# The last stage of a one-core encoder layer: the two expert rows of each token are added to x by accumulating transfers instead of by VectorE and GpSimd

## The reference, cut to what matters

```
    x = x + jnp.concatenate([dsa_out, ml_out], axis=-1) @ w_out[layer]
    x = x + memory_cross_attn(rmsnorm(x, norm_x_g[layer]), mem_n, ...)
    x = x + hier_moe(rmsnorm(x, norm_ffn_g[layer]), ...)
return rmsnorm(x, final_norm_g)
```

## Time and profile before

| | us |
|---|---|
| median of 3 runs | 2610.08 |
| the profiled execution | 2609.71 |
| its span, first to last instruction | 2607.9 |
| last expert store landed | 2554.86 |
| first `fin_o` tile finished | 2588.22 |
| last `fin_o` tile finished | 2603.58 |

### The profile page before, as it was taken

The page is one execution under the profiler, slowest core; times in us unless marked ns, Lnnn a source line. Parts: engine busy times, 40 slices in busy tenths (PEclk is TensorE's granted clock), DMA queues, the critical chain, the costliest instruction groups (busy, mean ns, idle before and its releaser), DMA issues.

```text
span 2607.9 us, 31347 instructions
## 1 busy us (share of the span) xinstructions
PE 2373.8 (91%) x11141; PEld 1866.7 (72%) x11141; DVE 1530.6 (59%) x1704; ACT 1214.9 (47%) x1376; POOL 305.7 (12%) x182
## 2 busy tenths in 40 slices
PE   6999999989999999999998299999999999999990
PEld 6888588667889998885887276666666666666660
DVE  4322376564335543223223488888888888888875
ACT  4222333354323442223222266776776777776751
POOL 0000000000000000000000112222222222222222
PEclk9999999999999999999999699999999999999995
DMA  4333133202424653320433489999999999999985
GB/s 174 97 96 97 48 92 95 71 25 91 147 93 147 177 181 126 97 89 1 120 96 118 144 309 400 410 402 394 410 395 394 413 404 395 407 398 400 402 331 215
DMA packets 141965, 580.45 MB, mean 223 GB/s; under 512 B 24395, under 2 KB 26705, under 8 KB 86737
## 3 DMA queue, kind: packets, MB, share of 16 engines
q1 hardware_dynamic: 136528, 562.85, 57.9%
q0 software_dynamic: 5376, 16.81, 2.0%
HBM read 571.15 MB, written 25.23 MB: 229 GB/s over the span
## 4 chain that ended last, share of the span: by engine, by line
PE 61%; DMA 17%; DVE 12%; issue 5%; ACT 4%; POOL 0%; DVEq 0%; SPq 0%; ACTq 0%; POOLq 0%
PE psd L726 42%; DMA e_raw<-in_w_gate_dram 8%; DMA e_raw<-in_w_down_dram 7%; DVE e_lo L1916 5%; PE psx L1052 3%; PE psx L1053 3%; PE psd L1080 2%; ACT e_hi L1430 2%; DVE y_sb L2025 1%; PE psd L987 1%; PE psx L1037 1%; PE psx L968 1%; PE psx L762 1%; PE psx L1060 1%; ACT y_sb L1474 1%
## 5 line engine op out<-in xcount | busy, mean ns | idle before, releaser
L1916 DVE TENSOR_TENSOR e_lo<-e_raw,e_hi 128x2048 fp32r<-128x2048 f32 x320 | 721.2, 2286 | 138.3 <-ACT e_hi L1430 136.0
L1535 DVE TENSOR_TENSOR w_lo<-w_raw,w_hi 128x1024 fp32r<-128x1024 f32 (+1 forms) x240 | 291.0, 1213 | 642.4 <-ACT w_hi L1130 642.3
L1430 ACT ACTIVATE e_hi<-e_raw 128x2048 fp32r<-128x2048 f32 x320 | 602.1, 1912 | 88.3 <-DMA e_raw<-in_w_gate_dram 65.3
L1130 ACT ACTIVATE w_hi<-w_raw 128x1024 fp32r<-128x1024 f32 (+1 forms) x240 | 252.0, 1050 | 763.9 <-PE psd L726 763.9
L1052 PE MATMUL psx<-e_hi,xt_pair 128*128 128x512 f32 x1024 | 430.1, 420 | 67.1 <-DVE e_lo L1916 61.5
L1053 PE MATMUL psx<-e_lo,xt_pair 128*128 128x512 f32 x1024 | 418.2, 408 | 0.0
L726 PE MATMUL psd<-w_hi,act_hi 128*128 128x512 f32 (+1 forms) x832 | 320.7, 385 | 6.1 <-DVE act_lo L1591 2.0
L726 PE MATMUL psd<-w_hi,act_lo 128*128 128x512 f32 (+1 forms) x832 | 319.7, 384 | 0.0
L726 PE MATMUL psd<-w_lo,act_hi 128*128 128x512 f32 (+1 forms) x832 | 319.6, 384 | 0.0
L1052 PEld LDWEIGHTS psx<-e_hi,xt_pair 128*128 128x128 f32 x1024 | 204.1, 199 | 138.9 <-DVE e_lo L1916 90.8
L661 POOL DMA_INDIRECT y_rows<-y_sb,put_idx x32 | 208.6, 6517 | 588.8 <-DVE y_sb L2025 588.8
(11 more groups left out here) (305 smaller groups left out, 2932.5 us busy)
## 6 DMA issues: line engine op xcount, KB each, us to landing
e_raw<-in_w_gate_dram SPq DMA_DIRECT2D x128, 1024.0 KB, 11.3
e_raw<-in_w_up_dram SPq DMA_DIRECT2D x128, 1024.0 KB, 7.9
e_raw<-in_w_down_dram SPq DMA_DIRECT2D x128, 1024.0 KB, 10.0
w_raw<-in_w_in_dram SPq DMA_DIRECT2D x72, 512.0 KB, 3.6
w_raw<-in_w_ckv_dram SPq DMA_DIRECT2D x64, 512.0 KB, 3.7
w_raw<-in_w_out_dram SPq DMA_DIRECT2D x32, 512.0 KB, 3.6
w_raw<-in_w_cq_dram SPq DMA_DIRECT2D x32, 512.0 KB, 3.6
w_raw<-in_w_co_dram SPq DMA_DIRECT2D x32, 512.0 KB, 3.6
```

The lines of the kernel that those rows point to most:

```text
L1130: act.activation(w_hi[j % 2][:, :, 0:w], w_raw[j % 4][:, :, 0:w], ACT.Copy).then_inc(hi_done, 1)
L1430: act.activation(e_hi[n][:, :], raw_at(b, r)[:, :], ACT.Copy).then_inc(e_hi_done, 1)
L1535: dve.tensor_tensor(w_lo[j % 2][:, :, 0:w], w_raw[j % 4][:, :, 0:w], w_hi[j % 2][:, :, 0:w].bitcast(F32), ALU.subtract).then_inc(lo_done, 1)
L1916: dve.tensor_tensor(e_lo[n][:, :], raw_at(b, r)[:, :], e_hi[n][:, :].bitcast(F32), ALU.subtract).then_inc(e_lo_done, 1)
```

## The change

The tiles `y_back` and the two engines' additions go. GpSimd itself begins eight transfers of 1 MB with `accum_op=ALU.add`: each reads 128 rows of `y_rows` and adds them to a tile of `x_res` in place. The first four bring the first experts' rows (k = 0), one for each tile; the second four bring the second experts' rows (k = 1), and each waits until the first transfer into its tile has landed, since both add to the same bytes. ACT's square of tile t waits for `back_land[t]` at 32, that is for both. DVE only norms. GpSimd needs no word from SP to begin; SP's only load is `fin_gain`.

```
-        y_back = [at(f"y_back{t}", [P, 2, D], 16 * t) for t in range(TT)]
...
-        f_pair, f_add, f_sq, f_out = (sem(s) for s in ("f_pair", "f_add", "f_sq", "f_out"))
+        f_sq, f_out = (sem(s) for s in ("f_sq", "f_out"))
...
             sp.dma_start(fin_gain[:, :], final_norm_g.rearrange("(a d) -> a d", a=1).to_broadcast([P, D])).then_inc(fg_land, 16)
             for t in range(TT):
-                sp.dma_start(y_back[t][:, :, :],
-                             y_rows.rearrange("(k t p) d -> t p k d", k=2, p=P)[t]).then_inc(back_land[t], 16)
-            for t in range(TT):
                 sp.wait_ge(f_out, t + 1)
...
             pool.sem_inc(experts_done, 1)
 
-            for t in range(1, TT):
-                pool.wait_ge(back_land[t], 16)
-                pool.tensor_tensor(y_back[t][:, 0, :], y_back[t][:, 0, :], y_back[t][:, 1, :], ALU.add).then_inc(f_pair, 1)
+            for k in range(2):
+                for t in range(TT):
+                    if k:
+                        pool.wait_ge(back_land[t], 16)
+                    pool.dma_start(x_res[:, t, :], y_rows[T * k + P * t:T * k + P * t + P, :],
+                                   accum_op=ALU.add).then_inc(back_land[t], 16)
...
             for t in range(TT):
-                act.wait_ge(f_add, t + 1)
+                act.wait_ge(back_land[t], 32)
                 if t:
                     act.wait_ge(f_sq, t)
...
-            for t in range(TT):
-                if t == 0:
-                    dve.wait_ge(back_land[t], 16)
-                    link(dve.tensor_tensor(y_back[t][:, 0, :], y_back[t][:, 0, :], y_back[t][:, 1, :], ALU.add))
-                else:
-                    dve.wait_ge(f_pair, t)
-                dve.tensor_tensor(x_res[:, t, :], x_res[:, t, :], y_back[t][:, 0, :], ALU.add).then_inc(f_add, 1)
-                if t:
-                    finish(t - 1)
+            for t in range(TT - 1):
+                finish(t)
             finish(TT - 1)
```

## The result

The changed kernel takes 2618.02 us, the median of 19 runs; the kernel before, run beside it 19 times, 2611.53. The ratio is 1.0025, with a 95% interval of 1.0018 to 1.0033: 6.5 us slower, 4.7 to 8.6 by the interval. The forecast was 2618.

A forecast was written before the change was run, and what follows sets the result against it. The last stage was taken as bound by loads for 20 us, then by DVE and GpSimd. From 2554.9, adding 3.1, 2.5, 39.7, 5.0, 0.5 and 10.3 gave a 2616.0 us span, a time of 2618, range 2602 to 2639.

The forecast's parts named there:

- terms 1, 2: Start of the last stage: 3.1 us for start and landing of a GpSimd transfer, 2.5 us for loading `fin_gain`.
- term 3: Eight 1 MB accumulates in the last stage, each 4.96 us, twice a plain copy's time: 39.7 us.
- term 4: Output stores ahead of the last accumulate put off its landing: 5.0 us for tiles 0 and 1, 0.5 for the third.
- term 5: From the last landing to the end: ACT's square, DVE's norm of one tile, the store and program end, 10.3 us.
- two units: Each 1 MB accumulate takes twice a copy's 2.48 us, 4.96 us, giving a time of 2618; chance 45%.
- The prediction's other estimate: Sixteen engines at about 16.2 GB/s each accumulate at 259 GB/s: 4.05 us an accumulate, a time of 2611.
- The hidden waits: Second transfers' waits for the first into their tile, and GpSimd's issues of about 1 us, hide behind 15 us of queued work.
- The rival that feared 6.9 us: GpSimd's instruction bounds the eight accumulates at 6.9 us each, 55.2 us in all, a time of 2630; chance 5%.
- The faster side: Each of the eight accumulates costs only a copy's 2.48 us, DVE bounds the rest, a time of 2598; chance 13%.
- The point where its sign turns: The change neither gains nor loses when the eight accumulates take 32.1 us, 4.0 us each.

The follow-up runs named there:

- e1: The changed kernel with the addition left out of its eight transfers, so they only copy: ratio 0.9948 to the kernel before, stage 39.5 us.
- e3: The kernel before, but GpSimd first adds the second experts' rows to the first's in HBM, SP loads the sums, DVE adds them to x: ratio 1.0010.
- e9: e1 with each copy writing its destination as the rounded float32 type, so each element is converted: transfers 2.49 us apart, stage 40.2 us.
- e11: The changed kernel, unchanged, profiled a second time: span 2614.7 us, stage 58.4 us.
- e5: e4 with no output store begun before tile 3 has its last accumulate: ratio 1.0007 to the kernel before, stage 57.6 us.
- e4: The changed kernel with four buffers for the normed tiles in place of two: ratio 1.0023 to the kernel before, stage 57.7 us.
- e2: The kernel before with all additions on DVE and none on GpSimd: ratio 0.9977 to the kernel before, stage 47.5 us.
- e6: e2 with `fin_gain` loaded behind the second pair of rows: 2605.2 us, ratio 0.9973 to the kernel before, stage 45.0 us.

## Why the prediction was right, term by term

| term | forecast | measured |
|---|---|---|
| last expert store | 2554.9 | 2558.9 |
| start, fixed time and `fin_gain` (terms 1, 2) | 5.6 | 6.1 |
| eight accumulates (term 3) | 39.7 | 39.2 |
| output stores among them (term 4) | 5.5 | 2.3 |
| last landing to the end (term 5) | 10.3 | 10.8 |
| the stage | 61.1 | 58.4 |
| span | 2616.0 | 2617.3 |

The measured second row is the first landing, 11.0 us after the expert stores (2570.18 less 0.28 of issue, less 2558.86), less one accumulate of 4.9.

**Term 3 decided it, and held.** I took two units between the bounds of one and three, from full occupancy in the earlier trace rows; it is 4.90 against 2.48, a ratio of 1.98. The rule of the Trainium skill, "Collectives: The Full Stack", section "The bandwidth ceiling: the fold count and why AG ≠ RS ≠ AR", a ratio of 1.93 for its collectives, agrees with the trace. The prediction's other estimate from that section of the Trainium skill, 32.35 GB/s over the two engines that it counts, so 16.2 each and 259 for sixteen, does not: the stretches show 213 to 223. e1 and e3 take away the queue, the number of packets and the destination as causes; e9 takes away the elements' handling at least where they are converted.

**The hidden waits were hidden.** GpSimd's first four accumulates took 3.69 us of its own time together and the others 0.86 each, about L649's 0.97 in the earlier trace rows, and 4.9 us lie between landings across the step from the first four to the second. The rival that feared 6.9 us is gone.

**The faster side was priced rightly.** It said 2595.7 for copies that add, 40.8 us behind the expert stores; e1, with copies that don't, has 39.5. The point where its sign turns, 32.1 us for eight, leaves out the 0.5 of term 4; with it it is 31.6, still 4.0 each.

**Term 4 was mis-sized.** I gave each store a unit ahead of the last landing. Only one fell there: the intervals are 4.9, 4.9 and 7.2. The first store was issued at 2596.39, took 10.4 us to land beside the accumulates and came in at 2606.8, just behind the last of them; the second landed later still. The changed kernel's two queues (GpSimd's q0, SP's q1: packets, MB, share) from 2597 to 2600 and from 2600 to 2606:

```profile
q0 software_dynamic: 88, 0.59, 95.1%
q1 hardware_dynamic: 7, 0.06, 4.7%
```

```profile
q0 software_dynamic: 104, 0.75, 59.7%
q1 hardware_dynamic: 120, 0.97, 39.9%
```

For 3.6 us after its issue the store hardly moved, and then the stores moved more bytes than the accumulates. I had let it begin at once. What holds it back at first stays open; e11 has the same (0.02 MB in the first 3.6 us). The prediction also has the first store begin 6.3 us after its tile's landing, where the parts of term 5 give 5.9; it began 6.9 after it (2596.39 - 2589.48), since about 1 us of tile 0's table load showed. e5 shows the size in another way: without any store the last landing is 1.9 us earlier.

**What I had not named:** the wait for a store before tile 2 may be scaled. Term 5 took it that the tile before the last is scaled by then, and term 4 that its store begins just before the last landing; its scaling ended at 2609.22, 2.7 us behind it. With a store that takes 10.4 us and two buffers DVE waited 4.14 us, and tile 3's sum, ready at 2608.5, was used at 2609.14. That is the 0.5 us in term 5, and e4 takes it away.

**The exact time was partly luck.** The stage came out 2.7 us shorter than forecast. The profile on which I built it had its last expert store 2.7 us earlier than the average of twelve. The two cancel. The difference between the kernels is the sounder figure: 8.1 us of stage forecast, 5.4 measured.

Where the gain went that the change aimed at: it does free the engines. DVE has nothing to do until 33 us into the stage. But each accumulate costs twice a copy, and the stage has little else to do while the accumulates run, so the transfer engines' work on the rows rose from 19.8 to 39.2 us, in a stage that had begun with a wait for just these engines. The loss that the earlier trace rows show on GpSimd and DVE is removed at less cost by e2 and e6.

## What to carry to other kernels

An accumulating transfer is an addition paid for in transfer time, twice the copy's. At the end of this kernel, where all data are waited for, it lost. It may pay where the engines are the bound and the transfer engines have room; no run here shows such a place. Before work is moved off an engine, ask what holds it: here it was another engine's additions beside it, and putting all of them on DVE, with the gain loaded behind the first rows, took 45.0 us for a stage that had taken 53.0. Count a last stage from the last event ahead of it, in both profiles: the sum of 2600 us ahead of it scatters by more than the effect.

## What the runs showed of the hardware

- An accumulate of 1 MB in float32 rows of 8 KB takes 4.9 us in a full queue, with its destination in SBUF (213 to 223 GB/s) or in HBM (219); a copy or a conversion to the rounded type 2.49 (418 to 434 in e1 and e9). Both have the same packets and counted bytes.
- SP's transfers beside GpSimd's accumulates move about as many bytes as these do (2.15 against 2.11 MB in 15 us of e3), which leaves them a third of the engines' time; the two kinds together reach 285 GB/s. A 1 MB store hardly moves for its first 3.6 us there and lands after 10.4 us, where it takes 3.9 alone; loads take 10.2 in the median.
- Two DVE products of one element per partition took 3.87 and 4.43 us while GpSimd added, each until GpSimd's addition of two operands was done, and 0.16 each in the changed kernel and in e2, where it doesn't add. A reciprocal, which reads one operand, took 0.17 beside the same addition.
- GpSimd's own time for a transfer of 1 MB is 0.53 us for a copy and 0.86 for an accumulate.
